# Six plain chunks instead of eight ahead of the first pair runs of a two-block transformer kernel

## What is computed

```python
def first_block(x, ...):                      # gMLP gate and convolution, then a feed-forward
    ...
    h = rms_norm(x, norm2_g)
    f = square(relu(h @ w_ff1))               # 1024 -> 4096
    x = x + f @ w_ff2                         # 4096 -> 1024
    return rms_norm(x, final_g)

def second_block(x, ...):                     # two attentions, then a feed-forward
    h = rmsnorm(x, g_pre_mix)
    q_a, k_a, v_a, q_i, k_i, w_i, q_d, k_d, v_d = split(h @ w_in)
    # rotary: concat([x1*cos - x2*sin, x2*cos + x1*sin]) on q_a, k_a, q_i, k_i, q_d, k_d
    ...                                       # top-k indexed attention, differential attention
    x = x + rmsnorm(y, g_post_mix)
    h = rmsnorm(x, g_pre_mlp)
    u = relu(h @ w_up)                        # 1024 -> 4096
    return x + rmsnorm((u * u) @ w_down, g_post_mlp)
```

## Time and profile before

| | |
|---|---|
| median of the runs | 1079.7 us |
| the profiled execution, its time | 1079.46 us |
| the profiled execution, its span | 1077.7 us |
| granted TensorE clock, mean over the span | 0.999 |
| TensorE matmul busy | 1063.9 us, 99% |
| VectorE, GpSimd, ScalarE busy | 65%, 62%, 37% |

### The profile page before, as it was taken

One profiled execution on the slowest core, in us unless ns is written; L12 is line 12 of the kernel. 1 busy time (PEld: TensorE's weight loads), 2 busy tenths in 40 slices (PEclk: granted clock), 3 DMA queues, 4 the chain that ended last, 5 costly groups with the idle time before them and its releaser, 6 DMA issues.

```text
span 1077.7 us, 17262 instructions
## 1 busy us (share of the span) xinstructions
PE 1063.9 (99%) x6163; PEld 932.3 (87%) x6163; DVE 702.3 (65%) x1382; ACT 400.5 (37%) x817; POOL 673.0 (62%) x460
## 2 busy tenths in 40 slices
PE   9999999999999999999999999999999999999997
PEld 6878888998899998889788787777899888999886
DVE  5999778961158864548689878676888113886033
ACT  5156565550016541220202346655765000465012
POOL 7979857577636677667556433135856763657762
PEclk9999999999999999999999999999999999999999
DMA  7422223244313243334443332112223932234512
GB/s 262 138 85 72 61 96 98 79 150 125 97 59 119 100 158 115 102 112 138 117 134 101 89 88 60 40 60 78 61 97 126 205 101 60 98 118 158 195 59 78
DMA packets 52251, 115.54 MB, mean 107 GB/s; under 512 B 21840, under 2 KB 22480, under 8 KB 52176
## 3 DMA queue, kind: packets, MB, share of 16 engines
q1 hardware_dynamic: 31200, 105.40, 30.1%
q10 hardware_dynamic: 20976, 9.15, 3.4%
HBM read 105.09 MB, written 4.19 MB: 101 GB/s over the span
## 4 chain that ended last, share of the span: by engine, by line
PE 82%; DVE 11%; ACT 3%; issue 2%; POOL 1%; DMA 0%; SPq 0%; DVEq 0%; ACTq 0%; POOLq 0%
PE bank L767 81%; DVE bank L2116 5%; PE bank L1294 1%; DVE tmp L2008 1%; DVE wl L2375 0%; ACT wh L1681 0%; POOL wl L568 0%; DMA x<-xT 0%; DVE gpad L2008 0%; DVE bank L2358 0%; PE bank L911 0%; DVE bank L2008 0%; DVE x L2189 0%; ACT probs L1831 0%; DVE bank L2360 0%
## 5 line engine op out<-in xcount | busy, mean ns | idle before, releaser
L568 POOL TENSOR_TENSOR wl<-raw,wh 128x1024 fp32r<-128x1024 f32 x140 | 334.0, 2386 | 11.7
L565 POOL TENSOR_SCALAR wh<-raw 128x1024 fp32r<-128x1024 f32 x139 | 148.8, 1071 | 230.2 <-PE bank L767 179.7
L767 PE MATMUL bank<-xh,wh 128*128 128x512 f32 (+2 forms) x747 | 256.9, 344 | 2.6 <-ACT vg L1575 1.5
L767 PE MATMUL bank<-xh,wl 128*128 128x512 f32 (+2 forms) x747 | 248.8, 336 | 0.0
L767 PE MATMUL bank<-xl,wh 128*128 128x512 f32 (+2 forms) x744 | 246.3, 338 | 0.3 <-DVE xl L2027 0.2
L767 PEld LDWEIGHTS bank<-xh,wh 128*128 128x128 f32 x747 | 142.1, 190 | 33.3 <-issue 19.5
L767 PEld LDWEIGHTS bank<-xl,wh 128*128 128x128 f32 x744 | 141.0, 190 | 13.8 <-DVE xl L2027 3.6
L767 PEld LDWEIGHTS bank<-xh,wl 128*128 128x128 f32 x747 | 142.3, 191 | 11.0
L1681 ACT ACTIVATE wh<-bank 128x512 fp32r<-128x512 f32 x96 | 52.2, 596 | 241.8 <-DVE bank L2360 103.1
L767 PE MATMUL bank<-uh,wh 128*128 128x512 f32 x320 | 123.1, 385 | 0.8 <-POOL ul L632 0.8
L767 PE MATMUL bank<-uh,wl 128*128 128x512 f32 x320 | 121.3, 379 | 0.0
(11 more groups left out here) (339 smaller groups left out, 2106.5 us busy)
## 6 DMA issues: line engine op xcount, KB each, us to landing
raw<-wstream SPq DMA_DIRECT2D x188, 512.0 KB, 3.5
x<-xT SPq DMA_DIRECT2D x8, 256.0 KB, 4.8
x4rows<-x_rows ACTq DMA_DIRECT2D x4, 512.0 KB, 7.7
out<-x4rows SPq DMA_DIRECT2D x8, 256.0 KB, 2.1
qd<-ropey ACTq DMA_DIRECT2D x16, 64.0 KB, 2.1
kd<-ropey ACTq DMA_DIRECT2D x16, 64.0 KB, 2.1
qa<-ropey SPq DMA_DIRECT2D x16, 64.0 KB, 2.0
ka<-ropey SPq DMA_DIRECT2D x16, 64.0 KB, 2.0
```

The costliest lines, as they stand in the source:

```text
L565: nc.gpsimd.tensor_scalar(wh[c][:], raw[c][:], 1.0, 1.0, ALU.mult, ALU.mult).then_inc(high_ready, 1)
L568: nc.gpsimd.tensor_tensor(wl[c][:], raw[c][:], wh[c][:].bitcast(F32), ALU.subtract).then_inc(split_ready, 1)
L767: return nc.tensor.matmul(out, stationary, moved, start=start, stop=stop)
```

## The change

`PLAIN` goes from 8 to 6, so that runs 0 and 2 have five pairs instead of four, behind six plain chunks. To have the t sums two chunks sooner, they are made in two sets of banks (4 and 5, 6 and 7) in turn, their rounding and remainders are two instructions of 512 columns in place of four of 256, and ScalarE evacuates all plain chunks. In the second block the scaled parts of the first round are made ahead of the last two squares, and the `row_scale` chain moves behind run 2. The weight slots of the first pair are counted from the run's end, so that its pieces become free in another order (`free_at`): the first sums of weights (role 1) go into the slot of the last plain chunk. The norm's transposes of the first block go to bank 5. `early_rope` writes its two sine products back into the banks and joins from there; banks are given back behind the joins.

```diff
-PLAIN = 8
+PLAIN = 6
-FIRST_BANK = (0, 2, 0, 1)
+FIRST_BANK = (3, 2, 3, 1)
 def slot_of(p, role):
-    return (PAIR_RUNS[run_of(p)][0] + role) % SLOTS
+    first, _, count = PAIR_RUNS[run_of(p)]
+    return (first + 2 * count + role) % SLOTS
+def free_at(p, role):
+    first = PAIR_RUNS[run_of(p)][0]
+    return first - SLOTS + (slot_of(p, role) - first) % SLOTS + 1
...
+        t_sides = [at("t_sides0", [P, 2, 2, 4, Q], F32R, behind), at("t_sides1", [P, 2, 2, 4, Q], F32R, tmp_at)]
+        t_banks = [(bank[4], bank[5]), (bank[6], bank[7])] * 2 + [(bank[6], bank[7]), (bank[4], bank[5])] * 2
+        def norm_bank(i):
+            return bank[5 if i == 5 else 7]
...
 # GpSimd, split_pair
                 if place_in(p) == 0:
-                    pool.wait_ge(chunk_done, n - 3)
+                    pool.wait_ge(chunk_done, free_at(p, 0))
...
 # TensorE, pair: the first pair of a run
                 if alone:
-                    pe.wait_ge(evacuated, e - 2)
+                    if run in (0, 2):
+                        pe.wait_ge(t_ready, 16 if run else 6)
...
 # ScalarE
             def scaled_parts(k, gain):
-                if k:
-                    act.wait_ge(t_ready, 4 * k - 2)
-                A(bank[4][:, EARLY], x[:, k % 4, EARLY], ACT.Copy, scale=col(gain, k % 4)).then_inc(scaled_part, 1)
-                act.wait_ge(t_ready, 4 * k)
-                A(bank[5][:, EARLY], x[:, 4 + k % 4, LATE], ACT.Copy, scale=col(gain, 4 + k % 4)
-                  ).then_inc(scaled_part, 1)
+                if k % 4 >= 2:
+                    act.wait_ge(t_ready, 2 * k - 2)
+                for b, part, columns in zip(t_banks[k], (k % 4, 4 + k % 4), (EARLY, LATE)):
+                    A(b[:, EARLY], x[:, part, columns], ACT.Copy, scale=col(gain, part)).then_inc(scaled_part, 1)
             def t_round(k):
                 act.wait_ge(t_made, 4 * k + 4)
-                for t, src in enumerate((bank[4][:, EARLY], bank[4][:, LATE], bank[5][:, EARLY], bank[5][:, LATE])):
-                    A(t_high[t][:, k % 4], src, ACT.Copy).then_inc(t_rounded, 1)
+                for sides, b in zip(t_sides, t_banks[k]):
+                    A(sides[:, :, 0, k % 4], two(b[:]), ACT.Copy).then_inc(t_rounded, 1)
             def sum_round(p, i):
                 if place_in(p) == 0:
-                    act.wait_ge(chunk_done, chunk_of(p) - 3 + role)
+                    act.wait_ge(chunk_done, free_at(p, role))
             def plain_tiles(c0, first, norm, k0, p, gain):
...
+                def evacuate(c):
+                    act.wait_ge(chunk_done, c0 + c + 1)
+                    act.wait_ge(ul_ready, first + c - 1) if c >= 2 else act.wait_ge(sq_added, 6 * KT if first else 2 * KT)
+                    A(two(sq[c % 2][:]), by_token(bank[c % 4][:]), ACT.Relu).then_inc(evacuated, 1)
...
+                if first:
+                    act.wait_ge(xl_ready, 5 * KT)
+                else:
+                    scaled_parts(k0, gain)
+                    act.wait_ge(xl_ready, 2 * KT)
+                    act.wait_ge(sq_added, 2 * KT)
+                scaled_parts(k0 + 1, gain)
+                t_round(k0)
+                evacuate(0)
+                t_round(k0 + 1)
+                scaled_parts(k0 + 2, gain)
+                squared(0)
+                evacuate(1)
+                scaled_parts(k0 + 3, gain)
+                t_round(k0 + 2)
+                squared(1)
+                evacuate(2)
+                t_round(k0 + 3)
+                squared(2)
...                                            # evacuate and square 3, then 4
+                norm_sd(norm)
+                sum_round(p, 0)
+                sum_round(p, 1)
+                evacuate(5)
+                squared(5)
+                sum_round(p, 2)
+                sum_round(p, 3)
...                                            # second block, loop over k of the squares
+                if k == KT - 1:
+                    act.wait_ge(xl_ready, 4 * KT + 6)
+                    act.wait_ge(bc_used, 13)
+                    scaled_parts(4, "pre_mlp")
...
-            scaled_parts(4, "pre_mlp")
 # VectorE, t_sums part 1: two remainders of 512 columns instead of four of 256; plain_run:
-                for c in range(4):
-                    t_sums(k0 + c, 0, gain)
-                    if c == 0:
-                        dve.wait_ge(sq_added, (6 if norm == 13 else 2) * KT)
-                    evacuate(c)
-                    t_sums(k0 + c, 1, gain)
-                    if c < 3:
-                        rest(c)
+                t_sums(k0, 0, gain)
+                t_sums(k0 + 1, 0, gain)
+                t_sums(k0, 1, gain)
+                t_sums(k0 + 1, 1, gain)
+                t_sums(k0 + 2, 0, gain)
+                rest(0)
+                t_sums(k0 + 2, 1, gain)
+                t_sums(k0 + 3, 0, gain)
+                rest(1)
+                t_sums(k0 + 3, 1, gain)
+                rest(2)
+                norm_total(norm)
+                dve.wait_ge(t_ready, 2 * k0 + 8)
+                weight_sums_first(p)
                 rest(3)
-                rest(4)
-                norm_total(norm)
-                weight_sums_first(p)
-                rest(5)
                 weight_rest(p, 0)
                 weight_rest(p, 1)
+                weight_sums_last(p)
+                rest(4)
                 norm_factor(norm)
-                weight_sums_last(p)
-                rest(6)
                 weight_rest(p, 2)
                 weight_rest(p, 3)
-                rest(7)
+                rest(5)
 # VectorE, early_rope
-                rope_first(g, C_QI + 2 * g, bank[(2 * g + 1) % 4])
-                rope_second(g, C_QI + 2 * g, bank[5 if g == 1 else (2 * g + 2) % 4])
-                rope_join(g, E_P2 + 1 + 2 * g)
+                mul(two(tmp[0][:, cs]), first, cosines).then_inc(first_rope, 1)
+                dve.wait_ge(first_rope, 2 * g + 1)
+                mul(first, first, sines).then_inc(first_rope, 1)
...                                            # the same for the second bank, in tmp[2]
+                V.tensor_tensor(two(ropey[:, g % 2, 1, cs]), two(tmp[2][:, cs]), first, ALU.add).then_inc(evacuated, 1)
+                V.tensor_tensor(two(ropey[:, g % 2, 0, cs]), two(tmp[0][:, cs]), second, ALU.subtract
+                                ).then_inc(evacuated, 1)
 # VectorE, second block
             plain_run(C_FF2, 13, 4, pairs_of(2)[0], "pre_mlp")
+            pair_run(2)
             dve.wait_ge(rn_ready, 14)
             link(mul(row_scale[:], rn[:, 0:TB], rn[:, 0:TB]))
...
-            pair_run(2)
```

More of the change, by code:

```diff
@@ L326, in build @@
                        for r in range(len(PAIR_RUNS))]
[L327 to L330, removed]
+        t_sides = [at("t_sides0", [P, 2, 2, 4, Q], F32R, behind), at("t_sides1", [P, 2, 2, 4, Q], F32R, tmp_at)]
+        t_high = [t_sides[i // 2][:, i % 2, 0] for i in range(4)]
+        t_low = [t_sides[i // 2][:, i % 2, 1] for i in range(4)]
         work = at("work", [P, TB, S], F32, behind)
@@ L726, in _ @@
             split_rounds(C_FF1 // SLOTS, (C_FF1 + PLAIN) // SLOTS)
+            for n in range((C_FF1 + PLAIN) // SLOTS * SLOTS, C_FF1 + PLAIN):
+                split_chunk(n)
             split_pairs(0)
@@ L737, in _ @@
             split_rounds(last_round + 1, (C_FF2 + 3) // SLOTS)
-            second_round = (C_FF2 + 3) // SLOTS
-            for n in range(second_round * SLOTS, second_round * SLOTS + SLOTS):
+            for n in range((C_FF2 + 3) // SLOTS * SLOTS, C_FF2 + PLAIN):
                 split_chunk(n)
@@ L1096, in _, with feed_norm @@
                 out1_last(o)
+            def feed_norm(i, squares):
+                pe.wait_ge(t_ready, 14 if i == 13 else 6)
+                norm_sums(i, ss, 0, sq_added, squares)
             def feed_first(c0, e0, xl0, i, squares, between=None):
@@ L1107, in feed_first @@
                     pe.wait_ge(evacuated, e0 + c - 3)
-                    hooks = {0: lambda: norm_sums(i, ss, 0, sq_added, squares)} if c == 5 else {}
+                    hooks = {0: lambda: feed_norm(i, squares)} if c == PLAIN - 1 else {}
                     chunk_transposed((c0 + c) % SLOTS, bank[c % 4][:], xh, xl, hooks=hooks)
@@ L1145, in pair @@
                 if alone and run in (0, 2):
-                    pe.wait_ge(t_ready, 32 if run else 16)
+                    pe.wait_ge(t_ready, 16 if run else 8)
                 if alone and run == 1:
@@ L1705, in plain_tiles, with squared @@
             def plain_tiles(c0, first, norm, k0, p, gain):
-                for c in range(PLAIN):
-                    if c < 4:
-                        t_round(k0 + c)
-                    if c >= 4:
-                        act.wait_ge(chunk_done, c0 + c + 1)
-                        act.wait_ge(ul_ready, first + c - 1)
-                        A(two(sq[c % 2][:]), by_token(bank[c % 4][:]), ACT.Relu).then_inc(evacuated, 1)
+                def evacuate(c):
+                    act.wait_ge(chunk_done, c0 + c + 1)
```

(12 more changed lines are left out.)

69 lines of the change are left out of this document (38 added, 31 removed).

## The result

The changed kernel takes 1083.4 us, the median of six runs (1083.26 to 1084.8), beside 1079.59 for the kernel before in the same runs: a ratio of 1.0038, 95% interval 1.0028 to 1.0048. It is slower, as the forecast's sum had it, but by 3.8 us and not by 1.8; the time lies above the range (1078.6 to 1082.9). The profiled execution took 1083.42 (span 1081.7), 3.96 more than the one of before.

The account below looks back on a forecast made before the run. VectorE, slower than TensorE in a pair, was taken to set the pair runs' ends through its first corners; losses of 0.5 and 1.3 us made 1.8, giving 1081.5 us on the median's scale, range 1078.6 to 1082.9.

Parts of the forecast that it names:

- the forecast's sum: Whole kernel: 0.5 lost in block 1 plus 1.3 in block 2, 1.8 us slower.
- What bounds the kernel: Pair runs: VectorE is slower per pair, 9.78 us; with enough lag a five-pair run ends 41.00 behind its first corner.
- Block 1, +0.5: Run 0: first corner at 190.1, end at 231.1 against 230.58, 0.5 us lost.
- The collisions: Block 1: two VectorE tile remainders wait for GpSimd's split of the next pair; corner at 190.1, floor 188.75.
- Block 2, +1.3: Run 2: first corner at 789.7, end at 830.8 against 829.51, 1.3 us lost.
- its term of 0.4 for the scaled parts: Block 2: early scaled parts delay squares and GpSimd's split by 0.8; TensorE waits 0.4 us before plain chunk 4.
- the four remainders that it saw blocked: Block 2, VectorE: tile remainders held by GpSimd's splits, ending at 773.9, 778.2, 783.7 and 787.9.
- The rounding that it let come out free: T sums: four instructions of 256 columns or two of 512 take the same time, no cost or gain.
- The row scale's 1.78: Block 2: the row_scale chain leaves the path ahead of run 2's first corner, 1.78 us won on VectorE.
- Rotary joins, costed at nothing: Rotary groups: joins from banks save VectorE 0.9 us, banks return about 1.5 later, TensorE works unbroken; no effect on time.
- The third rival: Rotary joins: VectorE's 0.9 us reaches the attention's end, 1080.6; no separate chance, counted within the 0.49 for same.
- the 0.9 which the prediction itself named for a lost cover: Rotary joins: if TensorE's unbroken work no longer covered them, the change would give 0.9 us.

Follow-up runs that it names:

- short subtracts: Changed kernel with GpSimd making the weights' low parts for 16 instead of 512 columns in the first two pairs of runs 0 and 2: 1080.78 us.
- the scaled parts back: Changed kernel with the scaled parts of round 4 put back behind the last two squares of block 2: 1082.98 us.

## Why the prediction was wrong

- **What bounds the kernel: right, with one gap.** Corners 9.78 apart and a run's end 41.0 behind the first corner held in the change, with the short subtracts and with the scaled parts back. But the distance from corner to end is not fixed: where a wait for GpSimd moved behind the corner it grew, to 31.97 from 31.22 with the row scale moved.
- **Block 1, +0.5: right** (0.58). The collisions are shown by the run with short subtracts. The Trainium skill's rule (SBUF — State Buffer, Who interferes with whom), that a VectorE instruction with two inputs in SBUF and a GpSimd instruction that reads SBUF exclude each other, holds in this trace: 1.74 against 0.68 for the same remainder.
- **Block 2, +1.3: right** (1.21), with its term of 0.4 for the scaled parts, which measured 0.5 when taken back. This was not luck: the four remainders that it saw blocked were to end at 773.9, 778.2, 783.7 and 787.9, and they ended, less the shift of 1.63, at 773.8, 778.4, 783.8 and 788.0. The rounding that it let come out free is slightly cheaper with wide instructions (1.06 for two of 512 columns, 1.21 for four of 256), which the sum did not need. The row scale's 1.78 was over-sized: the corner did come 1.79 earlier in the kernel before, but 0.75 of it was inherited by the next instruction, and 1.04 was won. In the changed kernel the sum of raw weights behind that corner takes 0.69, without a wait, so the forecast's sum did not suffer.
- **Rotary joins, costed at nothing: wrong, this is the step that failed.** It said that "TensorE asks for each of them four chunks (over 20 us) later; only the first two are asked for soon". That is the average of the ring, not the order of its next user. The natural projection takes a new bank every six matmuls (1.3 us) of its first chunk, so it reaches the sixth group's first bank at 552.0, 2.6 behind its own beginning; the old step gave that bank back at the sine product, 0.88 in time, the new one behind the join, at 552.85, 0.85 too late. The new step alone cost the kernel before 0.94, and the old step for this one group gave the change 1.0 back. The third rival looked at the same stage only for a gain.
- **The end of the span: not in the sum.** I set 1.8 us between span and time and never asked what ends the span. The length of a program was no cost in my reading; it was worth 1.1 of the span here, and 0.9 of the time in the kernel before with 17 instructions more.
- **The sum and the range.** 0.5 + 1.3 stood against 0.58 + 1.21; what lay outside were 0.99 and 1.1, both taken as zero with no upper end. A range that had carried the 0.9 which the prediction itself named for a lost cover, with the sign turned, would have reached 1083.8.

## What to carry to other kernels

When a buffer is given back later, find the very next instruction that takes it and the distance to that one, for the last turn of a loop above all, where the next user has another order. An instruction that stands blocked by GpSimd is not worth its length when it is moved: price what moves up into its place. And look at the end of the span in both traces before a difference of a microsecond is given to the change.

## What was not expected of the hardware

- VectorE's code comes in fetches of 8 KB through the DMA engines, about one for every 128 instructions. With 1839 instructions listed none fell near the end; with 1856 one fell among the last store's packets, which made the span 1.1 longer and the time 0.9; with 1857 SyncE still waited 0.5 longer, and with 1862 and more the fetch came earlier and cost nothing that these runs show. The Trainium skill (Advanced Engine Details and Errata, ISA Cache) speaks of lines of 16 KB, 256 instructions; the trace shows 16 KB for one of the two code queues and 8 KB for the one in question.
- A wait for GpSimd is handed on to the next instruction with two inputs in SBUF: when `row_scale` (1.23 us for 128x4, where the product behind it took 0.16) and the last remainder of block 1 (1.74 where it takes 0.68) were moved away, the sum of raw weights that came into their place took 0.75 longer in both cases.
- Eight rotary DMA issues on ScalarE took 5.03, 5.63 and 5.80 us in three kernels that differ only in the rotary step, but the step does not decide it: with that of the change they took 6.04 in the run with short subtracts. In these three longer ones the extra time sits almost wholly in one issue: 1.24, 1.30 and 1.57 in place of 0.61. In each a 16 KB fetch of code begins within 0.1 us of that issue's start (543.48 and 543.49, 543.32 and 543.38, 541.88 and 541.90); in the change it begins 0.35 behind the start of the issue that it meets, which takes 0.62. No run moved the fetch alone, so this stays a coincidence in time, and the cause is open.
